# A planned eight-core decoder layer: other transfer costs in the planner, the mask transfers put later, and the residual gate's products moved into the stage of tile 2

## The reference

```python
u = layer_norm(x) * (1.0 + scale[:, None]) + shift[:, None]   # shift, scale, gate = split(c @ w_ada + b_ada)
q, k, v, z_a, bg, cg, xin, z_c = jnp.split(jnp.einsum('bsd,de->bse', u, w_in), IN_SPLITS, axis=-1)
s = jnp.einsum('bhiqd,bhikd->bhiqk', q_blk, k) + bias          # T5 buckets of k - q, causal
p = softmax(s); a = p[:, :, 0] - lam * p[:, :, 1]              # two maps of each of 8 heads
o = einsum('bhqk,bhkd->bhqd', a, v); o = o * rsqrt(mean(o*o) + eps) * subln_gain
y_attn = o * silu(z_a)
y_conv = bg * conv3(cg * xin) * silu(z_c)
merged = g_a * (y_attn @ w_branch[0]) + g_c * (y_conv @ w_branch[1])   # g = sigmoid(u @ w_gate + b_gate)
return layer_norm(ALPHA * x + (1.0 + gate[:, None]) * (merged @ w_out), ln_gain, ln_bias)
```

## Time and profile before

| | |
|---|---|
| runs | 3613.71, 3620.47, 4127.85 us; median 3620.47 |
| the profiled execution | 3616.32 us, span 3614.8 on its slowest core (3607.0 to 3614.8) |
| busy, share of the span | PE 95%, DVE 74%, ACT 69%, POOL 5% |
| granted clock of PE, means of the cores | 0.986 to 0.988 |
| chain that ended last | PE 77%, issue 6%, DMA 5%, ACT 4%, DVE 4% |
| DMA | 624 MB, 173 GB/s over the span, one queue |

### The profile page before, as it was taken

One profiled execution on the slowest core, in us unless ns is written; L12 is line 12 of the kernel. 1 busy time (PEld: TensorE's weight loads), 2 busy tenths in 40 slices (PEclk: granted clock), 3 DMA queues, 4 the chain that ended last, 5 costly groups with the idle time before them and its releaser, 6 DMA issues.

```text
span 3614.8 us, 69302 instructions; the slowest of 8 cores (3607.0 to 3614.8 us)
## 1 busy us (share of the span) xinstructions
PE 3417.2 (95%) x18424; PEld 1331.6 (37%) x18780; DVE 2662.1 (74%) x5163; ACT 2486.5 (69%) x2905; POOL 187.9 (5%) x229
## 2 busy tenths in 40 slices
PE   7798889999999989999999999999999999999998
PEld 2343333333333333333333333333333333333334
DVE  4257878788788678776787785667777876876867
ACT  3355667787887675776677777676776777777772
POOL 1000100000000001000000000000000000000000
PEclk9899999999999999999999999999999999999999
DMA  9879997787798598666655665656555645655653
GB/s 289 186 207 228 211 183 179 198 225 163 208 253 208 135 252 212 136 165 143 184 151 137 163 171 123 147 138 178 142 132 155 174 127 142 181 132 138 173 122 119
DMA packets 395334, 624.42 MB, mean 173 GB/s; under 512 B 125739, under 2 KB 159659, under 8 KB 391500
## 3 DMA queue, kind: packets, MB, share of 16 engines
q1 hardware_dynamic: 394956, 619.96, 68.0%
HBM read 516.40 MB, written 103.41 MB: 171 GB/s over the span
## 4 chain that ended last, share of the span: by engine, by line
PE 77%; issue 6%; DMA 5%; ACT 4%; DVE 4%; SPq 2%; POOL 0%; ACTq 0%; DVEq 0%; POOLq 0%
PE ps L29 77%; ACT PBT L43 4%; SPq L160 2%; DVE QST L48 1%; DVE PBT L48 1%; DMA v_scr<-VS 1%; DMA out<-X 1%; DMA BIG<-wpk 1%; DMA TH<-rho_scr 1%; PE ps L33 0%; DMA kT_scr<-KS 0%; DMA BIG<-w_ss 0%; DMA q_scr<-QB 0%; DMA BIG<-w_g 0%; DMA X<-x_all 0%
## 5 line engine op out<-in xcount | busy, mean ns | idle before, releaser
L43 ACT ACTIVATE PBT<-ps 128x1024 bf16<-128x1024 f32 (+1 forms) x2112 | 2018.6, 1009 | 661.0 <-PE ps L29 525.1
L29 PE MATMUL ps<-PBT,V 128*128 128x512 bf16 (+6 forms) x4481 | 1209.8, 360 | 71.8 <-ACT PBT L43 34.1
L29 PE MATMUL ps<-BIG,W 128*128 128x512 bf16 (+1 forms) x4730 | 1235.5, 376 | 22.4 <-ACT W L43 3.0
L48 DVE TENSOR_TENSOR QST<-PBT 128x1024 bf16<-128x1024 bf16 x896 | 616.8, 689 | 420.0 <-ACT PBT L43 411.1
L29 PEld LDWEIGHTS ps<-BIG,W 128*128 128x128 bf16 x4864 | 455.1, 98 | 578.7 <-issue 91.2
L29 PE MATMUL ps<-Q,K 64*128 64x512 bf16 (+6 forms) x4608 | 645.1, 361 | 7.9 <-ACT PBT L43 7.5
L29 PEld LDWEIGHTS ps<-PBT,V 128*128 128x128 bf16 x4608 | 356.7, 97 | 714.9 <-issue 607.9
L48 DVE TENSOR_TENSOR QST<-QST 128x1024 bf16<-128x1024 bf16 x840 | 577.1, 687 | 34.0 <-DVE QST L48 0.9
L29 PE MATMUL ps<-UT,W 128*128 128x512 bf16 x1297 | 344.5, 381 | 9.4 <-ACT QB L43 4.3
L29 PEld LDWEIGHTS ps<-Q,K 64*128 64x128 bf16 x4608 | 144.9, 94 | 456.1 <-issue 441.5
L29 PE MATMUL ps<-W,UT 128*128 128x512 bf16 x866 | 234.4, 388 | 13.6 <-DVE SM L735 5.1
(11 more groups left out here) (134 smaller groups left out, 1897.0 us busy)
## 6 DMA issues: line engine op xcount, KB each, us to landing
W<-w_bf SPq DMA_DIRECT2D x688, 256.0 KB, 4.6
V<-v_scr SPq DMA_DIRECT2D x288, 256.0 KB, 5.3
K<-kT_scr SPq DMA_DIRECT2D x288, 256.0 KB, 4.8
UT<-wpk SPq DMA_DIRECT2D x80, 512.0 KB, 11.1
X<-x_all SPq DMA_DIRECT2D x52, 512.0 KB, 8.3
w_bf<-W SPq DMA_DIRECT2D x104, 256.0 KB, 12.3
TH<-rho_scr SPq DMA_DIRECT2D x63, 256.0 KB, 8.1
TH<-s_scr SPq DMA_DIRECT2D x63, 256.0 KB, 8.1
```

The costliest lines, as they stand in the source:

```text
L29: return lambda e: e.matmul(out(), lhsT(), rhs(), start=start, stop=stop)
L43: return e.activation(out(), in_(), func, **kw)
L48: return lambda e: e.tensor_tensor(out(), in0(), in1(), op)
```

## The change

In the planner: a DMA may carry a `load` of its own in place of its bytes (V stores 240000, stores of rho and s 108000, mask stores 240000, mask loads 480000, against 65536, 4096, 65536 and 65536). `BW` is 300 KB per us. `dlat` has five phases instead of three, with higher times between 250 and 470 us. What PE reads from another engine, and PSUM banks that another engine frees, become ready 0.2 us later (not for score products).

In the program: `masks2` is called once, behind both tiles, and its stores wait for tile 1's `uT_scr` store. `gate_g1` is called in the turn of tile 2, ahead of its convolution items, takes all its tiles from PST2, loads `w_g` in eight halves of 512 KB, and waits with all loads for a Q group of tile 3. `kvq[2]` counts 19.2 us more. The arithmetic is the same.

```diff
+        o.load = nbytes if load is None else load
 def simulate(g, nunits=200):
     LAT = 0.14
-    BW = 240e3
+    BW = 300e3
+    SLACK = 0.2
+    late = ("PSF", "PSE", "PSV")
     def dlat(o, t):
-        ph = 0 if t < 180.0 else 1 if t < 1450.0 else 2
+        ph = 0 if t < 60.0 else 1 if t < 250.0 else 2 if t < 470.0 else 3 if t < 1450.0 else 4
         if o.prio == 0 and o.nbytes == 1 << 18:
-            return 9.0
+            return (9.0, 9.0, 13.0, 9.0, 9.0)[ph]
         if o.prio == 0 and o.nbytes == 4096:
-            return (5.0, 7.0, 3.5)[ph]
+            return (5.0, 6.0, 11.0, 7.0, 3.5)[ph]
         if o.nbytes == 1 << 19:
-            return (5.5, 9.0, 5.5)[ph]
+            return (6.0, 8.5, 13.0, 9.0, 5.5)[ph]
         if o.prio >= 3:
-            return (4.5, 8.5, 4.0)[ph]
-        return (5.0, 7.0, 4.5)[ph]
+            return (4.5, 7.0, 12.0, 8.5, 4.0)[ph]
+        return (5.0, 7.0, 11.0, 7.0, 4.5)[ph]
...
-            st["dma"] = max(st["dma"], t + d) + o.nbytes / BW
+            st["dma"] = max(st["dma"], t + d) + o.load / BW
...
+            if ev[2] == 3:
+                o = g.ops[ev[1]]
+                for v in o.vbs:
+                    if v.pool.name in late:
+                        v.nd += 1
...
+                for s2 in o.succ:
+                    if s2.engs[0] == "pe" and s2.kind != "S":
+                        s2.nwait -= 1
+                        if s2.nwait == 0:
+                            mkready(s2)
...
+                slack = o.eng != "pe"
+                if slack:
+                    hpush(evs, (t + SLACK, o.seq, 3))
                 for v in o.vbs:
+                    if slack and v.pool.name in late:
+                        continue
...
                 for s2 in o.succ:
-                    if o.eng == "pe" and s2.engs[0] == "pe":
+                    if s2.engs[0] == "pe" and (s2.kind != "S" or o.eng == "pe"):
                         continue
...
-                              reads=[(fts[hg], 4 * hg + h) for h in range(4)] + [("uTs", 0)], writes=[("m", qd, hg)],
-                              prio=5)
+                              reads=[(fts[hg], 4 * hg + h) for h in range(4)] + [("uTs", 1)], writes=[("m", qd, hg)],
+                              prio=5, load=240000)
...
         def gate_g1():
-            cr, bg_ = VB(PST), VB(PST)
+            after = [SEQ["after"]]
+            cr, bg_ = VB(SEQ["st"]), VB(SEQ["st"])
...
-                for kq in range(2):
-                    w = bigvb()
+                for kq in range(4):
+                    w = VB(SEQ["st"])
+                    g.dma(w.ap, A(w_g[hc, kq].rearrange("p k c -> p (k c)")), reads=after, writes=[(w, 0)], prio=2,
+                          nbytes=1 << 19)
...
-                        g.op("pe", 0.9, MM(bf(vb), (lambda k=k: cr.ap()[:, k * 128:(k + 1) * 128]),
+                        g.op("pe", 1.2, MM(bf(vb), (lambda k=k: cr.ap()[:, k * 128:(k + 1) * 128]),
...
+        kvq[2] += 19.2
...
-            if j == 0:
-                masks2(fts, ft_)
+        masks2(fts, ft_)
...
                 ln_tile(2)
-                gate_g1()
                 halo_t()
...
                 SEQ["st"], SEQ["after"] = PST2, ("qe", j + 1, 4)
+                if j == 2:
+                    gate_g1()
```

More of the change, by code:

```diff
@@ L89 @@
                  "pair", "gate", "eng", "start", "end", "idx", "need", "sem", "val", "prev", "lat", "done", "sched",
-                 "nbytes", "deps0")
+                 "nbytes", "deps0", "load")
 class Graph:
@@ L100, in __init__, with op @@
         self.gate0 = 0.0
-    def op(self, engs, dur, fns, reads=(), writes=(), prio=5, kind="x", nbytes=0, lat=0.0):
+    def op(self, engs, dur, fns, reads=(), writes=(), prio=5, kind="x", nbytes=0, lat=0.0, load=None):
         o = Op()
@@ L157, in op, with dma @@
         return o
-    def dma(self, out, in_, reads=(), writes=(), prio=5, nbytes=65536):
-        return self.op("sp", 0.43, (lambda e: e.dma_start(out=out(), in_=in_())), reads, writes, prio, "dma", nbytes)
+    def dma(self, out, in_, reads=(), writes=(), prio=5, nbytes=65536, load=None):
+        return self.op("sp", 0.43, (lambda e: e.dma_start(out=out(), in_=in_())), reads, writes, prio, "dma", nbytes,
+                       load=load)
 def hpush(h, x):
@@ L194, in simulate @@
     LAT = 0.14
-    BW = 240e3
+    BW = 300e3
+    SLACK = 0.2
+    late = ("PSF", "PSE", "PSV")
     def dlat(o, t):
-        ph = 0 if t < 180.0 else 1 if t < 1450.0 else 2
+        ph = 0 if t < 60.0 else 1 if t < 250.0 else 2 if t < 470.0 else 3 if t < 1450.0 else 4
         if o.prio == 0 and o.nbytes == 1 << 18:
-            return 9.0
+            return (9.0, 9.0, 13.0, 9.0, 9.0)[ph]
         if o.prio == 0 and o.nbytes == 4096:
-            return (5.0, 7.0, 3.5)[ph]
+            return (5.0, 6.0, 11.0, 7.0, 3.5)[ph]
         if o.nbytes == 1 << 19:
-            return (5.5, 9.0, 5.5)[ph]
+            return (6.0, 8.5, 13.0, 9.0, 5.5)[ph]
         if o.prio >= 3:
-            return (4.5, 8.5, 4.0)[ph]
-        return (5.0, 7.0, 4.5)[ph]
+            return (5.0, 7.0, 12.0, 8.5, 4.0)[ph]
+        return (5.0, 7.0, 11.0, 7.0, 4.5)[ph]
     owner, lastvb = {}, {}
@@ L378, in simulate @@
                             mkready(s2)
+            if ev[2] == 3:
[3 more added lines that the diff above has]
+                        v.nd += 1
+                        if v.nd == v.nt:
+                            for u in v.pool.units[v.slot]:
+                                owner[u] = None
+                                lastvb[u] = v
+                                freed[u] = t
+                for s2 in o.succ:
[3 more added lines that the diff above has]
+                            mkready(s2)
             if ev[2] == 1:
@@ L533, in build_nc @@
     w_ss = din("w_ss", [8, 128, 2048])
-    w_g = din("w_g", [2, 2, 128, 4, 512])
+    w_g = din("w_g", [2, 4, 128, 2, 512])
     b_ada_col = din("b_ada_col", [128, 16])
@@ L878, in v_group @@
                                   "p (h d) -> p h d", h=4)),
-                              reads=[(vs, 0)], writes=[("v", hc, j, t, o)], prio=3, nbytes=1 << 16)
+                              reads=[(vs, 0)], writes=[("v", hc, j, t, o)], prio=3, nbytes=1 << 16, load=240000)
         def v_weights(hc):
@@ L1034, in head_norm @@
                 g.dma(A(rho_scr.ap()[j, h]), (lambda: hs.ap()[:, 8:12]), reads=[(hs, 1)], writes=[("rho",) + key],
-                      prio=0, nbytes=4096)
+                      prio=0, nbytes=4096, load=108000)
                 rb = VB(PTH)
@@ L1075, in head_norm @@
             g.dma(A(s_scr.ap()[j, h]), (lambda: hs.ap()[:, 20:24]), reads=[(hs, 4)], writes=[("s",) + key], prio=0,
-                  nbytes=4096)
+                  nbytes=4096, load=108000)
             sbv = VB(PTH)
@@ L1357, in masks2 @@
                           A(bass.AP(m_scr, qd * MSTR + 63, [[128, 64], [4 * MSTR, 8], [1, 64]])),
-                          reads=[("m", qd, 0), ("m", qd, 1)], writes=[("Mq", qd)], prio=3)
+                          reads=[("m", qd, 0), ("m", qd, 1)], writes=[("Mq", qd)], prio=3, load=480000)
             g.op("dve", 0.1, (lambda e: e.tensor_copy(lsm[:, 6:7], M[:, 0, 0:1])), [("Mq", q_) for q_ in range(4)],
@@ L1403, in gate_g1 @@
         def gate_g1():
-            cr, bg_ = VB(PST), VB(PST)
-            g.dma(cr.ap, A(c_rep.rearrange("p k n -> p (k n)")), writes=[(cr, 0)], prio=2, nbytes=1 << 19)
-            g.dma(bg_.ap, A(b_ada_g), writes=[(bg_, 0)], prio=2, nbytes=1 << 19)
+            after = [SEQ["after"]]
+            cr, bg_ = VB(SEQ["st"]), VB(SEQ["st"])
+            g.dma(cr.ap, A(c_rep.rearrange("p k n -> p (k n)")), reads=after, writes=[(cr, 0)], prio=2, nbytes=1 << 19)
+            g.dma(bg_.ap, A(b_ada_g), reads=after, writes=[(bg_, 0)], prio=2, nbytes=1 << 19)
             for hc in range(2):
                 vb = pse()
-                for kq in range(2):
-                    w = bigvb()
[L1411 to L1414, removed]
-                        g.op("pe", 0.9, MM(bf(vb), (lambda k=k: cr.ap()[:, k * 128:(k + 1) * 128]),
-                                           (lambda w=w, kk=kk: w.ap().rearrange("p a b -> p (a b)").bitcast(F32)[
-                                               :, kk * 512:(kk + 1) * 512]),
+                for kq in range(4):
+                    w = VB(SEQ["st"])
+                    g.dma(w.ap, A(w_g[hc, kq].rearrange("p k c -> p (k c)")), reads=after, writes=[(w, 0)], prio=2,
+                          nbytes=1 << 19)
+                    for kk in range(2):
+                        k = kq * 2 + kk
+                        g.op("pe", 1.2, MM(bf(vb), (lambda k=k: cr.ap()[:, k * 128:(k + 1) * 128]),
+                                           (lambda w=w, kk=kk: w.ap()[:, kk * 512:(kk + 1) * 512]),
                                            start=(k == 0), stop=(k == 7)), [(w, 0), (cr, 0)], [(vb, 0)], kind="F")
@@ L1571, in make_in_maps @@
     w_g = np.ascontiguousarray(
```

(2 more changed lines are left out.)

## The result

The changed kernel is slower, by about 1.2%: 3654.57 and 3665.58 us in its undisturbed runs, against 3612.29 to 3620.47 for the kernel before, ratio **1.0123** with a 95% interval of 1.0077 to 1.017.

What follows compares the result with a forecast made beforehand. TensorE, busy 95% of the span, was taken as the bound, with DMA as the second limit. Terms A to F, -3 - 15 - 8.8 + 0 + 4 + 0 = -22.8, took 3616.3 to 3593 us, range 3562 to 3625.

Steps and rivals of the forecast that it cites:

- F: All stages, reordered by the new lag and the transfer rate of 300: 0 us taken, between -10 and +10.
- B: Tile 1's transposes and V products, 104 to 164 us: moved masks and later statistics remove waits, -15 us (0 to -21).
- A: The start: the gate's 1 MB of loads, `c_rep` and `b_ada_g`, leaves it, -3 us (0 to -6).
- rival 1: Masks come late: DVE waits for M and the queue holds stores and weights, 3627 us; chance 0.08.
- C: Gate's products leave 277 to 300 us (22.9) and return as 14.1 of filler in tile 2's stage: net -8.8 us.
- E: Tile 2's stage and later weights: ten 512 KB loads displace eleven weight loads, +4 us (0 to +12).
- rival 3: The staged `w_g` halves land later and stall PE in tile 2's stage, +14 us, 3607; chance 0.07.
- D: Tile 1's stage, 300 to 508 us: longer planned transfer times against tight transfers, 0 us, between -15 and +15.
- Rival 2: Transfers hold the stage of tile 1, so its early gains shrink and the gate's 14.1 us are added: 3612; chance 0.16.
- Rival 4: Later stages gain too, the 0.2 us lag removing PE's waits on ACT and DVE: 3568 us; chance 0.13.

Runs made afterwards that it cites:

- kernel 1: Changed kernel with the planner's transfer rate back at 240 KB per us: ratio 0.9998 to before; 3583.1 us on full-clock cores (granted clock averaging 0.989 or more).
- kernel 6: Kernel before with only the mask transfers moved behind both tiles: ratio 0.999 to before, 3571.2 us on full-clock cores.
- kernel 5: Unchanged copy of the kernel before, run again: ratio 1.001, 3581.9 us on full-clock cores.
- kernel 7: Kernel before with only the gate's products moved to the stage of tile 2, in halves: ratio 1.0037 to before, 3602.4 us on full-clock cores.
- kernel 9: Changed kernel with rate 240 and the gate's products left where before has them: ratio 0.9986 to before, 3577.1 us on full-clock cores.
- kernel 12: Changed kernel with rate 240, run once more on the third chip: ratio 1.0006 to before, 3583.2 us on full-clock cores.
- kernel 10: Changed kernel with rate 240 and the first tile's x_own loads waiting for the gate, freeing both ST slots: ratio 1.0003 to before, 3579.3 us on full-clock cores.
- kernel 8: Changed kernel with rate 240 and the landing-time table of the kernel before: ratio 1.0078 to before, 3596.9 us on full-clock cores.
- kernel 4: Changed kernel without the 0.2 us lag, rate 300 kept: ratio 1.0136 to before, 3607.0 us on full-clock cores.

## Why the prediction was wrong

**The step that failed is F.** It took the new order of everything else as 0, between -10 and +10, "a tenth of it either way" of the idle time after 508 us. The transfer rate, one part of that order, measured +45 in the changed kernel and +23 on the kernel before. Instead of nothing, readers of transfers that ACT and DVE met too early held the two engines for 85 to 110 us together between 508 and 1500, and PE's idle time there doubled. Two things went wrong in F. I bounded the cost by the idle time that was there, which bounds a gain but not a loss: a worse order can make any amount of new idle time. (The 99 us were too many besides: they were read on core 4, with its missing records; core 0 idles 62.5 there, 41 and 21.5.) And the size of the rate had a row in my own table: the stage from 300 to 508 moved 211 GB/s at a DMA share of 0.98, and the 100 us near the last first-use loads 231 at 0.91. By these a core would get 215 to 255 when transfers are dense (an estimate: 211 / 0.98 and 231 / 0.91), and 300 lies above that. It isn't one number: kernel 1's stretch from 900 to 1060 would give 282 (251 / 0.89), and of the stages in the tables only the first 60 us reached 300. That I left the sign open ("nothing says which sign") overlooked this. The Trainium skill, page "HBM Reference", section Specifications (TRN2), gives some 358 GB/s for each core of a pair, by which 300 would be safe. This case's rows disagree (246 at a DMA share of 0.98, of loads and stores mixed), and the measurement decides. The mechanism itself, a reader placed too early that holds an engine, I had used in B for the statistics on DVE.

**A and B** were right in mechanism. Tile 1's V ends 20.45 us earlier, without a wait over 1 us. Idle PE up to 164 us falls by 15 (forecast: 18 for both). On its own B is worth 11 at the end on full-clock cores (kernel 6). Moving the gate, which frees A's ST slots, takes some 9 us of idle time off these 164 us on the kernel before (kernels 5 and 7, medians of the cores with all records), but only 1 or 2 once the masks have moved (kernels 9 and 12): A and B mostly recover the same time. The opposite result, rival 1, is refuted: DVE doesn't wait for M.

**C and E** have the wrong sign together with A's share: forecast -3 - 8.8 + 4, some -8; measured +6 (kernels 9 and 12) and +20 (kernels 5 and 7). C took its gain from the wait of 7.21 and the slower second half. In kernel 9, with the masks, the table and the lag but the gate left, there is no such wait to be saved. The products take some 16 us in five pieces between K, Q and attention of tile 0, with no wait in front of any, and the last 16 run as fast as the first half in the earlier trace rows:

```profile
266.37 7.06 PE L29 MATMUL ps<-BIG,ST 128*128 128x512 f32 x16
```

In kernel 12 they come back as some 16 us from 630 us on, and idle time from 164 to 508 is 37 on core 1, against 38 in kernel 9. So C came to about nothing there. On the kernel before the wait for `w_g` is saved (6.1 us on core 1 of kernel 5), and yet idle time from 164 to 508 is 32 to 37 in kernel 7 against 25 to 32; what it consists of stays open. E's price for the displaced weights held: 7 measured, +6 forecast for that part; the 2 that should come back in the stage of tile 2 were 5 more lost there. That is rival 3's place, with a smaller price than its 14, and its mechanism, lateness of the halves, doesn't carry it: PE waits for none of them in kernel 12, and two more slots change little (kernel 10). The rule of the Trainium skill that I had weighed here (page "DMA: Bandwidth & Descriptors", section Measured, on transfers that GpSimd issues, where these are SyncE's) is not settled by that, since no kernel varies the size of `w_g`'s loads alone. The halves land after 7.6 us in the changed kernel, a whole after 13.8.

**D** was set at 0. The first transposes of tile 3 did come some 65 us earlier (442.0 against 506.9 on core 0), as its better branch says, though idle PE from 164 to 508 didn't fall (35 to 40); the granted clock there rose from 0.93 to 0.96. The table gains some 14 us (kernels 1 and 8) where the rate is right. Rival 2 is refuted by the same mark. **Rival 4** was right that the lag gains, at 240; at 300 no gain shows (kernel 4).

The prediction named its own failure: a shift as large as forecast at tile 3's transposes, and no earlier end, means that the later stages lost it. That is what happened.

What stays open: the parts do not add up. Masks, table and lag each gain 11 us or more on full-clock cores in one comparison, yet kernel 9, which has all three, is 5 us under before by the ratio and 7 on those cores. The new loads of V, rho, s and mask transfers are in every kernel made from the changed one and were not tried alone, so they may cost. And each edit of the planner's costs makes another order of the whole program, so that a difference of 0.4% between two of them is not the price of the line edited unless the idle time of the stage shows it.

## What to carry to other kernels

In a kernel whose order is fixed by a plan, a transfer rate above what a core gets can be dear, because the reader of a late transfer holds its whole engine and all that is queued behind it. Read the rate from long stages with a DMA share near 1.0, not from the fastest 60 us. When an engine is said to wait for another, look at what that one waited for just before: the transfer showed only in ACT's and DVE's rows.

## What the runs showed of the hardware

The granted clock has, besides 1.00 (2.4 GHz), a level that some cores hold for 100 us and more at full load, here in pairs. In the profiled run of kernel 1, the following rows are of core 0 and of core 3:

```profile
140.00:250.00 110.00, 107.38 (x414) 43.75 (x412) 17.76 (x40) 35.88 (x54) 2.19 (x4) 0.80 0.75 186
```
```profile
140.00:250.00 110.00, 102.41 (x547) 47.76 (x546) 36.20 (x98) 50.05 (x72) 2.74 (x5) 0.97 0.93 229
```

On core 0 every microsecond of 160 to 180 shows 0.81 with PE busy throughout, and 16 products took 4.38 us instead of 3.62. It is neither of the two levels of 1.2 and 2.4 GHz. The Trainium skill (page "TensorE: Matmul & The Clock Gate", section Seeing it yourself) tells of a peak-current limiter that takes a whole die to 13/16 of the clock once three of its cores run dense matmuls. The level agrees with the 0.81. That it takes a whole die isn't so in this run: cores 2 and 3 of that die had 0.98 and 0.97 in the same 110 us, and averaged 0.992 and 0.991 over the run. Ahead of it both cores look alike: from 60 to 140 us both have a granted clock of 0.88, and PE is busy 67.4 and 68.6 us. Cores 0 and 1 ended at 3610 and 3615, core 3 at 3580. Which cores it takes changes from run to run, in the kernel before too, and the slowest core sets the time. So some 20 to 30 us of a run can come from it, and the table gives full-clock cores beside the ratios. The changed kernel, which idles more, also has a lower mean clock from 508 to 1500 us (0.98 against 1.00), and none of its cores reaches 0.989. What sets it off here wasn't found.
